# Compressing the past in eight units of two sequences, with pages issued without a loop and the bias from unsplit weights

## The chip, the cores and the metric

The kernel runs on one core of one Trainium2 chip. Five engines work at once on their own queues and meet at semaphores: TensorE (PE, matmuls), VectorE (DVE), ScalarE (ACT), GpSimd (POOL) and SyncE (SP, here an issuer of transfers). The metric is the device time of one execution in microseconds (us), less is better.

## What is computed

One inference step of a four-layer decoder for a prompt of 256 tokens and eight sequences with eight new tokens each, in float32. Four token mixers stand between eight feed-forward networks; their weights stream through the core once. This case is about one part of the last mixer (sparse attention): the eight sequences' past, 1024 rows each in pages of 128, is compressed to 63 keys and 63 values a sequence and group.

```python
def _nsa_compress(kf, w1, pe, w2):
    ...
    n_cmp = (tk - NSA_CMP_LEN) // NSA_CMP_STRIDE + 1
    sub = kf[:, :n_sub * NSA_CMP_STRIDE].reshape(b, n_sub, NSA_CMP_STRIDE, g, d)
    hid = 0.0
    for m in range(n_parts):
        rows = slice(m * NSA_CMP_STRIDE, (m + 1) * NSA_CMP_STRIDE)
        part = jnp.einsum('bnpgd,pdh->bngh', sub + pe[rows][:, None, :], w1[rows])
        hid = hid + part[:, m:m + n_cmp]
    return jax.nn.gelu(hid) @ w2

    past = cache_nsa_kv[page_table].reshape(b_s, past_len, 4, NSA_KV_HEADS, HEAD_DIM)
    ...
    k_cmp = _nsa_compress(full[:, :, 0], cmp_w1[0], cmp_pe[0], cmp_w2[0])
    v_cmp = _nsa_compress(full[:, :, 1], cmp_w1[1], cmp_pe[1], cmp_w2[1])
```

A hidden layer of 256 over windows of 32 rows (16 pairs of rows of 128 numbers), a gelu, and a second layer. The position term `pe` is the same for all windows, so its product with `w1` is a bias of the hidden layer.

## The kernel before, in words

The program does the past first, then x and the twelve stages, each of which takes its weights from one stream of chunks (`L264` issues one, `L290` and `L299` split it on ACT and DVE, `L317` multiplies). Matmuls run on float32r operands, so each float32 operand is split into a high part (a copy on ACT, rounded as it is written) and a low part (the remainder, on DVE), and a product is three matmuls: high with high, low weights with high, high weights with low.

The past is done in four *units*: unit 0 the keys and unit 1 the values of the first four sequences, units 2 and 3 those of the other four. A unit needs its pages (eight per sequence, 128 KB each) in `staged_pages`. SP issues those of sequences 0, 1 (and 4, 5), POOL those of 2, 3 (and 6, 7), both in a loop that reads a page number into a register and issues one transfer (`stage_pages`, `L1375` to `L1377`). `act_pairs` and `dve_pairs` turn the pages of a unit into `pair_hi` and `pair_lo`, four instructions of 512 columns a sequence pair on each engine; there are two slots, and unit u takes slot u modulo 2. `hidden_of` multiplies: two halves `ht` of the hidden layer, 16 row pairs, three products, 504 columns (63 windows, two groups, four sequences), 96 matmuls a unit. `act_gelu_past` adds the bias and takes the gelu out of PSUM, `keys` and `values` are the second layer on PE in plain float32 (two instructions a matmul), and `act_keep_past` copies their results.

The first-layer weights `w1` come in four pieces, by kind and by half of the hidden layer (16 row pairs of 128 columns); `act_w1_hi` and `dve_w1_lo` split each in two instructions. The bias is made on DVE in `dve_past`: 128 steps of 128 columns on the split weights, four accumulators in turn, between the pairs of unit 1 and those of units 2 and 3. Four matmuls with one column (`L1459`) sum it over the partitions, ACT copies it, and unit 2 waits for that copy.

The order of the work is written out by hand on each engine: `sp_past_first` and `sp_past_rest`, `pool_past`, `pe_past`, `act_past` (in three parts, with the scaling of x and the first weight splits between them) and `dve_past`. Stream chunks land where the pages of sequences 0 and 1 stood, the split weights where slot 0 stood, and `x_hi` where the pages of sequences 2 and 3 stood, so those steps wait for the units that read there.

## Time and profile before

| | us |
|---|---|
| median of 3 runs (lowest, highest) | 2662.05 (2661.71, 2663.11) |
| the profiled execution | 2664.5 |
| its span in the profile | 2662.8 |
| first matmul of the past | 39.66 |
| first matmul of the weight stream | 151.77 |
| PE busy over the span | 2534.2 (95%) |

The profile is of one execution. A timeline row gives an instruction's start in us from the start of the span, its length, engine, line, operation, what it writes and reads, and, in brackets, how long its engine stood idle ahead of it and what ended that. Buffer numbers are left out, so the four pieces of `w1` all read `w_raw`, `w_hi` and `w_lo`, as the stream's chunks do; the line tells them apart. Lengths of matmuls overlap: what one costs in a row of many is the distance between starts. PEld is the loading of weights.

### The profile page before, as it was taken

To read this page: it belongs to the slowest core of one execution; us is meant where nothing else is said; L and a number is where in the kernel's file an instruction comes from. 1 tells how busy PE (TensorE), PEld (TensorE's weight loads), DVE (VectorE), ACT (ScalarE), POOL (GpSimd) and SP (SyncE) were. 2 spreads that over 40 slices of the span, in tenths; PEclk is the share of its full clock that TensorE was granted. 3 is DMA by queue.
4 is the path that set the end of the run, shared out by engine and by line. 5 is a ranking of instruction groups with operands and counts; after the bars stand their busy time and mean duration, and the time that the engine had idled before them with its cause. 6 is when DMAs were issued, how large, how long until landed. Compare 5 with 4: busy or idle time off the path is not lost. (4 is left out here: it accounts for less than half of the span.)

```text
span 2662.8 us, 49610 instructions
## 1 busy us (share of the span) xinstructions
PE 2534.2 (95%) x17087; PEld 2450.5 (92%) x17087; DVE 1425.2 (54%) x2311; ACT 1327.5 (50%) x1979; POOL 790.3 (30%) x803
## 2 busy tenths in 40 slices
PE   4899998999999997999999999999999998889998
PEld 3799997999999995999999998999999997669998
DVE  5734545645455457555455456554454445756453
ACT  4445544455365436565366433564365333755552
POOL 2623312333133212333133214333133211113331
PEclk9999999999999997999999999999999998989999
DMA  7224344344444341344443443334444453214432
GB/s 221 70 95 157 135 150 145 111 158 139 152 151 146 142 185 37 111 150 146 146 158 142 146 154 143 140 144 150 150 144 156 146 216 111 64 47 143 156 137 106
DMA packets 73977, 366.13 MB, mean 137 GB/s; under 512 B 9154, under 2 KB 29954, under 8 KB 36482
## 3 DMA queue, kind: packets, MB, share of 16 engines
q1 hardware_dynamic: 72210, 356.58, 37.6%
q0 software_dynamic: 1536, 4.20, 0.5%
q10 hardware_dynamic: 144, 4.19, 0.4%
q8 instruction: 55, 0.90, 0.1%
q14 instruction: 32, 0.26, 0.0%
HBM read 361.98 MB, written 4.92 MB: 138 GB/s over the span
## 5 line engine op out<-in xcount | busy, mean ns | idle before, releaser
L317 PE MATMUL bank<-x_hi,w_hi 128*128 128x320 f32 x3336 | 1036.3, 311 | 0.0
L317 PE MATMUL bank<-x_lo,w_hi 128*128 128x320 f32 x3336 | 1032.0, 309 | 0.0
L317 PE MATMUL bank<-x_hi,w_lo 128*128 128x320 f32 x3336 | 1031.9, 309 | 0.0
L290 ACT ACTIVATE w_hi<-w_raw 128x1024 fp32r<-128x1024 f32 (+1 forms) x641 | 657.7, 1036 | 743.0 <-PE bank L317 724.2
L299 DVE TENSOR_TENSOR w_lo<-w_raw,w_hi 128x1024 fp32r<-128x1024 f32 (+1 forms) x641 | 828.7, 1328 | 263.9 <-ACT w_hi L290 263.9
L317 PEld LDWEIGHTS bank<-x_hi,w_hi 128*128 128x128 f32 x3336 | 626.5, 188 | 2.1 <-issue 0.7
L317 PEld LDWEIGHTS bank<-x_hi,w_lo 128*128 128x128 f32 x3336 | 626.5, 188 | 1.3
L317 PEld LDWEIGHTS bank<-x_lo,w_hi 128*128 128x128 f32 x3336 | 626.5, 188 | 0.0
L317 PE MATMUL bank<-h_hi,w_hi 128*128 128x320 f32 x1664 | 518.3, 311 | 8.9 <-POOL h_lo L843 6.5
L317 PE MATMUL bank<-h_hi,w_lo 128*128 128x320 f32 x1664 | 517.3, 311 | 0.0
L317 PE MATMUL bank<-h_lo,w_hi 128*128 128x320 f32 x1664 | 517.2, 311 | 0.0
L501 POOL TENSOR_TENSOR h<-silu,up 128x320 f32<-128x320 f32 x176 | 222.2, 1263 | 842.2 <-DVE up L430 837.2
L317 PEld LDWEIGHTS bank<-h_hi,w_hi 128*128 128x128 f32 x1664 | 315.0, 189 | 10.1 <-POOL h_lo L843 7.3
L317 PEld LDWEIGHTS bank<-h_hi,w_lo 128*128 128x128 f32 x1664 | 315.1, 189 | 0.0
L317 PEld LDWEIGHTS bank<-h_lo,w_hi 128*128 128x128 f32 x1664 | 314.8, 189 | 0.0
L488 POOL TENSOR_TENSOR sq<-x 128x320 f32 (+1 forms) x104 | 105.9, 1018 | 592.6 <-DVE x L450 591.9
L430 DVE TENSOR_TENSOR up<-bank,rstd 128x320 f32<-128x320 f32 x176 | 86.3, 492 | 303.2 <-PE bank L317 303.2
L430 DVE TENSOR_TENSOR gate_in<-bank,rstd 128x320 f32<-128x320 f32 x192 | 93.6, 491 | 271.1 <-PE bank L317 262.7
L506 POOL TENSOR_TENSOR h_lo<-h,h_hi 128x320 f32 x176 | 237.3, 1366 | 0.0
L375 ACT ACTIVATE x_hi<-x,gains (+1 forms) x96 | 53.4, 563 | 211.2 <-DVE x L450 206.9
L391 ACT ACTIVATE h_hi<-h 128x320 f32 x176 | 81.6, 464 | 96.5 <-POOL h L501 96.5
L450 DVE SCALAR_TENSOR_TENSOR x<-bank,x 128x320 f32 (+1 forms) x96 | 47.0, 490 | 142.0 <-PE bank L317 142.0
(283 smaller groups left out, 1936.0 us busy)
## 6 DMA issues: line engine op xcount, KB each, us to landing
w_raw<-stream SPq DMA_DIRECT2D x289, 1024.0 KB, 4.8
w_raw<-stream SPq DMA_DIRECT2D x32, 768.0 KB, 4.1
n_sel<-pool_sel SPq DMA_DIRECT2D x64, 128.0 KB, 2.2
w_raw<-cmp_w SPq DMA_DIRECT2D x4, 1024.0 KB, 7.5
pages<-pool_cmp POOLq DMA_DIRECT2D x32, 128.0 KB, 2.4
pages<-pool_cmp SPq DMA_DIRECT2D x32, 128.0 KB, 2.1
w_new<-cmp_w ACTq DMA_DIRECT2D x1, 4096.0 KB, 13.7
const<-const SPq DMA_DIRECT2D x1, 1533.0 KB, 8.0
```

Source lines behind the costliest of these rows:

```text
L290: act.activation(w_hi[:, (2 * n + half) % HALVES, 0:k, :], raw[:, n % RAW, 0:k, P * half:P * half + P], ACT.Copy).then_inc(hi_ready, 2 if ...
L299: dve.tensor_tensor(w_lo[:, s, 0:k, :], raw[:, n % RAW, 0:k, P * half:P * half + P], w_hi[:, s, 0:k, :].bitcast(F32), ALU.subtract).then_i ...
L317: mm = pe.matmul(acc, w[:, s, kk, :], a[:, k0 + kk, :], start=(first and kk == 0 and w is w_hi and a is act_hi), stop=(last and kk == k - ...
L375: act.activation(x_hi[:, bass.ds(m, 1), :], x[:, bass.ds(m, 1), :], ACT.Copy, scale=gains[:, norm, bass.ds(m, 1)]).then_inc(xhi_ready, 1)
L391: act.activation(h_hi[:, bass.ds(2 * i + f, 1), :], h[:, f:f + 1, :], ACT.Copy).then_inc(hhi_ready, 1)
L430: dve.tensor_tensor(dst, bank[g % BANKS][:, 0:T], rstd[:, :], ALU.mult).then_inc(evacuated, 1)
L450: dve.scalar_tensor_tensor(out=xm, in0=bank[g % BANKS][:, 0:T].rearrange("p (a t) -> p a t", a=1), scalar=scale, in1=xm, op0=ALU.mult, op1 ...
L488: pool.tensor_tensor(sq[:, :].rearrange("p (a t) -> p a t", a=1), x[:, bass.ds(m, 1), :], x[:, bass.ds(m, 1), :], ALU.mult).then_inc(ssum_ ...
L501: pool.tensor_tensor(h[:, f, :], silu[:, f, :], up[:, f, :], ALU.mult).then_inc(prod_ready, 1)
L506: pool.tensor_tensor(h_lo[:, t, :], h[:, f:f + 1, :], h_hi[:, t, :].bitcast(F32), ALU.subtract).then_inc(hlo_ready, 1)
```

## The change

The past is done in eight units of two sequences: units 2q and 2q + 1 are the keys and values of sequences 2q and 2q + 1, with SP issuing the even sequence's pages and POOL the odd one's. There are four pair slots, and unit u takes slot u modulo 4; slots 2 and 3 stand where the raw `w1` lay, so ACT waits for the bias steps before it fills them. A hidden matmul has 252 columns, and a unit still 96 of them, in two parts `c` of eight row pairs. `w1` is cut by kind and by row pairs, so that a piece is 8 KB a partition in one stretch. `stage_pages` reads its eight page numbers first and then issues eight transfers, without a loop. The bias is made from the raw weights, 256 columns wide, 16 steps for the keys and 16 for the values, each on the sum of the step before. PE starts with 24 matmuls on `w1_hi0` into a bank that is not read. Each `keys` or `values` is four matmuls of 128 columns and stands between the two parts of a later unit; hidden values have their own room for keys and values.

```diff
         def stage_pages(engine, q, i):
+            of_batch = [engine.value_load(pages[0:1, NPAGES * (2 * q + i) + r:NPAGES * (2 * q + i) + r + 1], min_val=0, max_val=n_pages - 1)
+                        for r in range(NPAGES)]
+            if q >= 2:
+                engine.wait_ge(pair_lo_ready, 2 * (2 * q - 3) + i + 1)
+            for r, pg in enumerate(of_batch):
+                engine.dma_start(staged_pages[q % 2][:, i, r:r + 1, :],
+                                 A["pool_cmp"][bass.ds(pg, 1)].rearrange("a p n -> p a n")).then_inc(staged[2 * (q % 2) + i], 16)
...
+        def sp_w1(sp, k):
+            sp.dma_start(w1_raw[k][:, :, :], A["cmp_w1"][:, k // 2, 8 * (k % 2):8 * (k % 2) + 8, :]).then_inc(past_w1_landed[k], 16)
...
             sp.wait_ge(pages_landed, 16)
-            for b in range(2):
-                stage_pages(sp, 0, b)
-            sp_w1(sp, 1)
+            stage_pages(sp, 0, 0)
+            for k in range(1, 4):
+                sp_w1(sp, k)
             sp.dma_start(cmp_pe[:, :, :], A["cmp_pe"]).then_inc(cmp_landed, 16)
+            stage_pages(sp, 1, 0)
             sp.dma_start(w2z[:, :, :, :, :], A["cmp_w2"]).then_inc(w2_landed, 16)
...
+        def hidden_of(pe, unit, c):
+            kv, slot, k = unit % 2, unit % 4, 2 * (unit % 2) + c
+            pe.wait_ge(w1_lo_ready, 2 * k + 2)
+            for ht in range(2):
+                out, col = bank[(2 * unit + ht) % 6][:, 0:4 * N_CMP_S], slice(P * ht, P * ht + P)
+                if c == 0 and unit >= 3:
+                    pe.wait_ge(hid_gelu, PRIME + 2 * (unit - 3) + ht + 1)
+                for pp in range(8):
+                    at = slice(4 * c, 4 * c + 4 * N_CMP_S)
+                    for w, a in ((w1_hi, pair_hi), (w1_lo, pair_hi), (w1_hi, pair_lo)):
+                        mm = pe.matmul(out, w[k][:, pp, col], a[slot][:, pp, at],
+                                       start=(c == 0 and pp == 0 and w is w1_hi and a is pair_hi),
+                                       stop=(c == 1 and pp == 7 and a is pair_lo))
...
+            pe.wait_ge(w1_hi_ready, 2)
+            for pp in range(24):
+                pe.matmul(bank[7][:, 0:256], w1_hi[0][:, pp % 8, 0:P], w1_hi[0][:, pp % 8, :], start=True, stop=True)
...
+            for unit in range(8):
+                pe.wait_ge(pair_lo_ready, 2 * unit + 2)
+                hidden_of(pe, unit, 0)
+                if unit == 2:
+                    pe.wait_ge(bias_step, 32)
...
+                if unit >= 3:
+                    if unit % 2:
+                        keys((unit - 3) // 2)
+                    else:
+                        values((unit - 4) // 2)
+                hidden_of(pe, unit, 1)
+            values(2)
+            keys(3)
+            values(3)
...
         def act_pairs(act, unit):
-            if unit >= 2:
-                act.wait_ge(hid_ready, 2 * (unit - 2) + 2)
+            if unit in (2, 3):
+                act.wait_ge(bias_step, 16 * (unit - 1))
+            if unit >= 4:
+                act.wait_ge(hid_ready, 2 * (unit - 4) + 2)
...
+        def dve_bias(dve, kv):
+            dve.wait_ge(cmp_landed, 16)
+            acc = bias_part[:, kv, :]
+            for pp in range(16):
+                src, pe_of = w1_raw[2 * kv + pp // 8][:, pp % 8, :], cmp_pe[:, kv, pp:pp + 1]
+                if pp == 0:
+                    dve.tensor_scalar(acc, src, pe_of, None, ALU.mult).then_inc(bias_step, 1)
+                else:
+                    dve.wait_ge(bias_step, 16 * kv + pp)
+                    dve.scalar_tensor_tensor(out=acc, in0=src, scalar=pe_of, in1=acc, op0=ALU.mult, op1=ALU.add)\
+                        .then_inc(bias_step, 1)
...
+            dve_w1_lo(dve, 0)
+            dve_pairs(dve, 0)
+            for k in range(1, 4):
+                dve_w1_lo(dve, k)
+            dve_pairs(dve, 1)
+            for kv in range(2):
+                dve_bias(dve, kv)
+                dve_pairs(dve, 2 + kv)
+            for unit in range(4, 8):
                 dve_pairs(dve, unit)
...
+                act_w1_hi(act, 0)
+                act_pairs(act, 0)
+                for k in range(1, 4):
+                    act_w1_hi(act, k)
+                for unit in range(1, 4):
                     act_pairs(act, unit)
                 act.wait_ge(bias_summed, 1)
...
-                    sp.wait_ge(pair_lo_ready, 12 + n + 1)
+                    sp.wait_ge(pair_lo_ready, 10 + n + 1)
```

Two places of the order. First SP, at the start of the program; `TENSOR_LOAD` reads a page number, `DMA` issues a transfer. Before, with a loop body that runs eight times:

```order
L1385 DMA page_table_66<-pages 1x64
L1382 DMA w1_raw0_121<-cmp_w1 128x16x128
L1382 DMA w1_raw1_122<-cmp_w1 128x16x128
L1376 TENSOR_LOAD page_table_66
L1376 ISA x2
L1377 ISA
L1377 DMA pages01_129<-pool_cmp 128x256
L1375 REGISTER_ALU
L1375 COMPARE_AND_BRANCH
```

With the change, where the two rows of the number and the two of the page stand eight times each:

```order
L1387 DMA page_table_66<-pages 1x64
L1384 DMA w1_raw0_129<-cmp_w1 128x2048
L1375 TENSOR_LOAD page_table_66
L1375 ISA x2
L1380 ISA
L1380 DMA pages01_133<-pool_cmp 128x256
L1384 DMA w1_raw1_130<-cmp_w1 128x2048
L1384 DMA w1_raw2_131<-cmp_w1 128x2048
L1384 DMA w1_raw3_132<-cmp_w1 128x2048
L1393 DMA cmp_pe_70<-cmp_pe 128x32
```

One piece of `w1` instead of two is issued ahead of the first batch, the page numbers are read in one go, and the other three pieces go out behind one batch, not two.

Then DVE, from the first weights to the pairs of the unit that follows the bias; `w1_lo` are remainders of weights, `pair_lo` those of pages. Before, where the step on four accumulators goes on for 128 instructions:

```order
L1489 TENSOR_TENSOR w1_lo0_117<-w1_raw0_121,w1_hi0_113 128x1024 x2
L1489 TENSOR_TENSOR w1_lo1_118<-w1_raw1_122,w1_hi1_114 128x1024 x2
L1498 TENSOR_TENSOR pair_lo0_128<-pages01_129,pair_hi0_127 128x512 x4
L1498 TENSOR_TENSOR pair_lo0_128<-pages23_130,pair_hi0_127 128x512 x4
L1489 TENSOR_TENSOR w1_lo2_119<-w1_raw2_123,w1_hi2_115 128x1024 x2
L1489 TENSOR_TENSOR w1_lo3_120<-w1_raw3_124,w1_hi3_116 128x1024 x2
L1498 TENSOR_TENSOR pair_lo1_126<-pages01_129,pair_hi1_125 128x512 x4
L1498 TENSOR_TENSOR pair_lo1_126<-pages23_130,pair_hi1_125 128x512 x4
L1517 TENSOR_SCALAR bias_part_131<-w1_hi0_113,cmp_pe_70 128x128
L1520 SCALAR_TENSOR_TENSOR bias_part_131<-w1_lo0_117,cmp_pe_70,bias_part_131 128x128
L1520 SCALAR_TENSOR_TENSOR bias_part_131<-w1_hi0_113,cmp_pe_70,bias_part_131 128x128
L1498 TENSOR_TENSOR pair_lo0_128<-pages01_129,pair_hi0_127 128x512 x4
```

With the change:

```order
L1496 TENSOR_TENSOR w1_lo0_117<-w1_raw0_129,w1_hi0_113 128x1024 x2
L1505 TENSOR_TENSOR pair_lo0_122<-pages01_133,pair_hi0_121 128x512 x4
L1496 TENSOR_TENSOR w1_lo1_118<-w1_raw1_130,w1_hi1_114 128x1024 x2
L1496 TENSOR_TENSOR w1_lo2_119<-w1_raw2_131,w1_hi2_115 128x1024 x2
L1496 TENSOR_TENSOR w1_lo3_120<-w1_raw3_132,w1_hi3_116 128x1024 x2
L1505 TENSOR_TENSOR pair_lo1_124<-pages01_133,pair_hi1_123 128x512 x4
L1515 TENSOR_SCALAR bias_part_135<-w1_raw0_129,cmp_pe_70 128x256
L1518 SCALAR_TENSOR_TENSOR bias_part_135<-w1_raw0_129,cmp_pe_70,bias_part_135 128x256 x7
L1518 SCALAR_TENSOR_TENSOR bias_part_135<-w1_raw1_130,cmp_pe_70,bias_part_135 128x256 x8
L1505 TENSOR_TENSOR pair_lo2_126<-pages23_134,pair_hi2_125 128x512 x4
L1515 TENSOR_SCALAR bias_part_135<-w1_raw2_131,cmp_pe_70 128x256
L1505 TENSOR_TENSOR pair_lo3_128<-pages23_134,pair_hi3_127 128x512 x4
```

The pairs of unit 0 need one row of four instructions and stand ahead of three of the four weight pieces, and the bias is cut in two with the pairs of unit 2 between the halves.

## Rows read from the trace of the kernel before

**Rows 1.** Timeline, PE, 0 to 152 us: start us, length us, engine, line, operation, tiles, shape, count.

```profile
39.66 0.79 PE L1423 MATMUL bank<-pair_hi,w_hi 128*128 128x504 f32 x1 [39.66 <-DVE pair_lo L1498]
...
43.45 0.39 PE L1423 MATMUL bank<-pair_hi,w_hi 128*128 128x504 f32 x1
...
52.30 0.39 PE L1423 MATMUL bank<-pair_hi,w_hi 128*128 128x504 f32 x1
...
86.76 1.10 PE L1459 MATMUL bank<-one_col,bias_part 128*128 128x1 f32 x8 [1.44 <-DVE bias_part L1520]
...
119.84 3.71 PE L1450 MATMUL bank<-w2z,past_hid 128*63 128x128 f32 x32
...
151.77 0.42 PE L317 MATMUL bank<-x_hi,w_hi 128*128 128x320 f32 x1
```

**Rows 2.** Two stretches: length, busy us of each engine, PEclk, DMA share, GB/s.

```profile
0.00:39.60 39.60, 0.00 (x0) 0.00 (x0) 12.95 (x14) 15.61 (x16) 8.98 (x21) 1.00 0.79 224
...
85.30:94.70 9.40, 1.11 (x9) 1.02 (x9) 9.40 (x15) 6.78 (x8) 9.40 (x1) 0.62 0.00 1
```

**Rows 3.** Timeline, PE, 399.7 to 402.1 us, inside the weight stream.

```profile
399.80 0.31 PE L317 MATMUL bank<-x_hi,w_hi 128*128 128x320 f32 x1
...
402.00 0.31 PE L317 MATMUL bank<-x_hi,w_hi 128*128 128x320 f32 x1
```

**Rows 4.** Timeline, weight loads of PE (PEld), 85 to 88 us.

```profile
86.76 1.01 PEld L1459 LDWEIGHTS bank<-one_col,bias_part 128*128 128x128 f32 x8 [1.88 <-DVE bias_part L1520]
```

**Rows 5.** Timeline, SP, three windows of one batch of pages each.

```profile
4.78 12.75 SPq L1377 DMA_DIRECT2D pages<-pool_cmp  x8
...
2238.71 3.99 SPq L1584 DMA_DIRECT2D n_sel<-pool_sel  x8
...
2248.11 4.49 SPq L1584 DMA_DIRECT2D n_sel<-pool_sel  x8
```

**Rows 6.** Timeline, POOL, 0 to 130 us: its first page and its eighth.

```profile
4.01 0.71 POOL L1377 DMA_DIRECT2D pages<-pool_cmp  x1 [3.40 <-issue]
...
14.74 0.54 POOL L1377 DMA_DIRECT2D pages<-pool_cmp  x1 [0.98 <-issue]
```

**Rows 7.** The page's DMA issues: count, KB each, median us to landing.

```profile
w_raw<-stream SPq DMA_DIRECT2D x289, 1024.0 KB, 4.8
...
w_raw<-cmp_w SPq DMA_DIRECT2D x4, 1024.0 KB, 7.5
...
pages<-pool_cmp POOLq DMA_DIRECT2D x32, 128.0 KB, 2.4
...
pages<-pool_cmp SPq DMA_DIRECT2D x32, 128.0 KB, 2.1
```

**Rows 8.** Groups of 0 to 152 us: count | busy us, mean ns | idle before.

```profile
L1480 ACT ACTIVATE pair_hi<-pages 128x512 fp32r<-128x512 f32 x32 | 35.2, 1195 | 36.2 <-DMA pages<-pool_cmp 23.3 <-PE bank L1423 12.9
...
L1498 DVE TENSOR_TENSOR pair_lo<-pages,pair_hi 128x512 fp32r<-128x512 f32 x32 | 34.1, 1149 | 16.9 <-ACT pair_hi L1480 16.9
...
L1520 DVE SCALAR_TENSOR_TENSOR bias_part<-w_lo,cmp_pe,bias_part 128x128 f32<-128x128 f32 x64 | 17.9, 333 | 0.0
...
L1489 DVE TENSOR_TENSOR w_lo<-w_raw,w_hi 128x1024 fp32r<-128x1024 f32 x8 | 9.3, 1222 | 8.1 <-ACT w_hi L1470 8.1
...
L423 DVE SCALAR_TENSOR_TENSOR x_lo<-x,gains,x_hi 128x320 fp32r<-128x320 f32 x8 | 8.1, 1079 | 0.7 <-ACT x_hi L375 0.7
...
L1531 ACT ACTIVATE past_hid<-bank,cmp_bias 128x504 f32<-128x504 f32 x8 | 5.1, 679 | 25.2 <-PE bank L1450 13.0 <-PE bank L1423 10.1 <-PE bank L1441 2.1
...
L1531 ACT ACT_TABLE_LOAD x1 | 1.3, 1283 | 0.0
```

**Rows 9.** Groups of the whole span, DVE: a wide and a chained instruction.

```profile
L547 DVE SCALAR_TENSOR_TENSOR x<-x,gains,rstd 128x320 f32<-128x320 f32 x8 | 3.8, 548 | 0.0
...
L1953 DVE SCALAR_TENSOR_TENSOR n_hit<-n_imp,n_low,const 128x14 f32<-128x14 f32 x8 | 1.9, 234 | 0.3
```

More of the change, by code:

```diff
@@ L1279, in program @@
             staged = [sem(f"staged{b}") for b in range(4)]
+            past_clear = sem("past_clear")
             w1_hi_ready = sem("w1_hi_ready")
@@ L1413, in hidden_of @@
-        def hidden_of(pe, unit, ht, out):
-            kv = unit % 2
-            hi, lo = pair_hi[unit % 2], pair_lo[unit % 2]
-            for pp in range(16):
-                if unit < 2:
-                    if pp % 8 == 0:
-                        pe.wait_ge(w1_lo_ready, 4 * kv + 2 * ht + pp // 8 + 1)
-                at = slice(8 * (pp // 8), 8 * (pp // 8) + 8 * N_CMP_S)
-                for w, a in ((w1_hi, hi), (w1_lo, hi), (w1_hi, lo)):
-                    mm = pe.matmul(out, w[2 * kv + ht][:, pp, :], a[:, pp % 8, at], start=(pp == 0 and w is w1_hi and a is hi),
-                                   stop=(pp == 15 and a is lo))
-            return mm
@@ L1427, in pe_past @@
-        def pe_past(pe):
-            def unit(u, then=(None, None)):
-                pe.wait_ge(pair_lo_ready, 4 * u + 4)
-                if u == 3:
-                    pe.wait_ge(hid_gelu, PRIME + 2)
-                for ht in range(2):
-                    hidden_of(pe, u, ht, bank[(2 * u + ht) % 6][:, 0:8 * N_CMP_S]).then_inc(hid_ready, 1)
-                    if then[ht]:
-                        then[ht](u - 2)
-            def keys(half):
-                pe.wait_ge(hid_gelu, PRIME + 4 * half + 2)
-                pe.wait_ge(cmp_kept, PRIME + 2 * half - 1)
+            for q in range(4):
+                stage_pages(pool, q, 1)
@@ L1442, in keys @@
                                    start=(k == 0), stop=(k == 3))
                 mm.then_inc(cmp_made, 1)
-            def values(half):
-                pe.wait_ge(hid_gelu, PRIME + 4 * half + 4)
-                pe.wait_ge(cmp_kept, PRIME + 2 * half)
-                for b in range(4):
-                    for k in range(4):
-                        mm = pe.matmul(bank[7][0:N_CMP_S, P * b:P * b + P],
-                                       past_hid[:, k // 2, k % 2, N_CMP_S * b:N_CMP_S * b + N_CMP_S],
-                                       w2z[:, 1, k // 2, k % 2, :], start=(k == 0), stop=(k == 3))
-                mm.then_inc(cmp_made, 1)
@@ L1455, in pe_past @@
-            unit(0)
-            unit(1)
-            pe.wait_ge(bias_step, 128)
-            for k in range(4):
-                mm = pe.matmul(bank[6][:, k:k + 1], bias_part[:, k, :], one_col[:, :], start=True, stop=True)
-            mm.then_inc(bias_summed, 1)
-            pe.wait_ge(w2_landed, 16)
-            pe.wait_ge(bias_ready, 1)
-            unit(2, (keys, values))
-            unit(3, (keys, values))
-        def act_w1_hi(act, kv):
-            for ht in range(2):
-                act.wait_ge(past_w1_landed[2 * kv + ht], 16)
-                for c in range(2):
-                    act.activation(w1_hi[2 * kv + ht][:, 8 * c:8 * c + 8, :], w1_raw[2 * kv + ht][:, 8 * c:8 * c + 8, :], ACT.Copy)\
-                        .then_inc(w1_hi_ready, 1)
@@ L1473, in act_pairs, with values @@
-        def act_pairs(act, unit):
-            if unit >= 2:
-                act.wait_ge(hid_ready, 2 * (unit - 2) + 2)
-            for b in range(4):
-                act.wait_ge(staged[b], 16 * NPAGES * (unit // 2 + 1))
-                out, src = pairs_of(pair_hi[unit % 2], b), staged_of(unit, b)
+            def values(q):
+                pe.wait_ge(hid_gelu, PRIME + 4 * q + 4)
+                pe.wait_ge(cmp_kept, PRIME + 2 * q)
+                for k in range(4):
+                    mm = pe.matmul(bank[7][:, 0:P], past_hid[:, 1, k // 2, k % 2, :], w2z[:, 1, k // 2, k % 2, :],
+                                   start=(k == 0), stop=(k == 3))
+                mm.then_inc(cmp_made, 1)
```

160 lines of the change are left out of this document (79 added, 81 removed).

## The prediction

> **What bounds the kernel now.** I read the stretches first, then TensorE's (PE) timeline, then what each wait on it ends on. Everything the change touches lies before 151.77 us, where the first matmul of the weight stream starts [rows 1]; after it the program is unchanged, so only that start can move. PE does nothing until 39.66 and stands nearly empty from 85.30 to 94.70 [rows 1, 2]; the rest of the stretch is matmuls without a break. The first gap ends on `pair_lo` from VectorE (DVE), which needs all four sequences' pages; the second ends on `pair_lo` of unit 2, which DVE makes only after the whole bias chain. So the stretch has three prices: a late head, a gap in the middle, and the matmuls themselves.
>
> **The matmuls.** 384 of 504 columns become 768 of 252. Thirty-nine starts of 504 columns cover 8.85 us [rows 1], 0.227 each; fifteen starts of 320 columns cover 2.20 us [rows 3], 0.147 each. The line through both, 0.436 ns a column, gives 0.117 us at 252. That is one bound. The other is the weight load, for the number of loads doubles: eight loads with one-column matmuls took 1.01 us [rows 4], so at most 0.126 each. I take 0.117, since at 0.147 and 0.227 the load is wholly hidden and the stream still (barely) exceeds it. 768 x 0.117 = 89.9 us against 384 x 0.227 = 87.2: 2.7 us dearer, or 9.6 by the other bound. A unit of 96 matmuls is 11.2 us. Keys and values were four groups, now eight of 4 matmuls with 128 columns; 16 such matmuls (32 instructions) took 3.71 us [rows 1], so 0.93 a group.
>
> **The head.** A batch of eight pages took SP 12.75 us in the loop. The same work without a loop stands at the end of the trace: eight issues in 3.99 us, and 2248.11 - 2242.70 = 5.41 us of reading eight page numbers ahead of the next eight [rows 5]: 9.4 us. POOL's first page went out at 4.01 [rows 6]; one page number (5.41 / 8 = 0.68) earlier, at 3.3, the table was there. SP's batch is then issued by 12.7 and lands 2.1 later [rows 7], at 14.8. POOL's: its loop spaced pages by (14.74 - 4.01) / 7 = 1.53 us [rows 6]; without the loop eight issues cost between SP's 4.0 and 8 x 1.53 - 5.4 = 6.8, since its number reads may take no less. Landing takes 2.4, so 15.1 to 18.0; I take 16.5. Unit 0 needs these two batches alone, not four. ScalarE (ACT) then needs two instructions of 35.2 / 32 = 1.10 us, DVE two of 34.1 / 32 = 1.07 [rows 8]: PE starts at 20.8 instead of 39.66. The weights of w1 now come in 8 KB rows, the shape of a stream chunk, which lands in 4.8 us where the old 512-byte rows took 7.5 [rows 7]; the three later ones are issued from 12.7 on, and DVE wants the last at about 24. I cost them at nothing while that holds. The 24 added warm-up matmuls run before 20.8 on an idle PE; I give them no gain, because PE idles again between them and the first pages. The first nine matmuls took 3.79 us where nine later ones take 2.04 [rows 1]; I keep these 1.75 us.
>
> **The bias chain and the gap.** 128 instructions on the split weights (64 of them 17.9 us [rows 8]) become 32 of twice the width on the raw ones. But there were four accumulators in turn, and now each instruction waits for the one before it. Width 256 lies two thirds of the way from 333 ns (128 wide, [rows 8]) to 548 (320 wide, [rows 9]): 0.476, plus 0.3 / 8 = 0.04 for a wait on DVE's own last result [rows 9]: 0.516. Pipelined it would be 17.9 / 64 = 0.28 and 3.8 / 8 = 0.475, so 0.41. I take 0.516 because the wait is in the code: 16 steps are 8.3 us for each of keys and values. The raw weights lie under slots 2 and 3, so ACT may fill those slots only after each half of the chain; queued behind that wait on ACT are pairs(3), the bias copy and gelu(0).
>
> Walked through, on DVE: 20.8; six weight remainders of 9.3 / 8 = 1.16 [rows 8] to 27.8; pairs(1), 4 x 1.07, to 32.1; bias of the keys to 40.4; pairs(2), where ACT does 4 x 1.10 and DVE 2 x 1.07 behind it, to 46.9; bias of the values to 55.2; pairs(3) to 61.7. On PE: unit 0 from 20.8 to 33.8 (cold start included), unit 1 to 45.0, a wait of 1.9 for pairs(2), first half of unit 2 to 52.5, a wait of 2.7 for the bias, the four bias matmuls 1.0 [rows 4], second half to 61.8. Unit 3 finds its pairs; gelu(0), after ACT's pairs(3) at 59.6, a table load of 1.28 and half of 0.68 [rows 8], frees its bank at 61.6. Units 3 to 7 at 11.2 + 0.93 follow without a wait, because ACT and DVE need 6.5 us for the pairs of a unit that lasts 12.2: 122.7. Two values groups, one keys group, and a gelu of 0.68 between: 126.2. The x work (DVE 8.1 us, [rows 8]) and the first weight splits hide behind units 6 and 7; if that cover were gone they would cost up to these 8.1. The page issues of the later batches wait for pairs(1) and pairs(3), 20 us before use: nothing.
>
> **Sum.** The stream starts at 126.2 instead of 151.77: 25.6 us less. The profiled execution took 2664.5 us (span 2662.8); 2664.5 - 25.6 = 2638.9. The median of the runs, 2662.05, lies 2.4 below that execution, so I predict 2636. No change can be told from 0.2%, 5.3 us.
>
> **Rivals.**
> A, *the head is bound by transfer, not by issue*. The first 39.6 us moved 224 GB/s with the DMA engines 0.79 busy [rows 2]. If 224 stays, four weight pieces and the first two batches, 6 MB, are in at 28. Taken in the order of issue only the last weights are late: pairs(1) and the chain behind it slip by some 4 us, 2640. If all share alike, unit 0 starts at 32: 2647. For it: the busy share; against it: nearly half of that traffic was w1 in 512-byte rows. 0.15.
>
> B, *POOL's pages come no faster unrolled*: 1.53 us a page stays and the number reads come on top, 3.3 + 5.4 + 12.3 + 2.4 = 23.4 instead of 16.5. Then the change does not do what it says on one of two queues, 2643. 0.07.
>
> C, *slower: the weight load stands beside the short matmul, not under it*. Place: the hidden layer's line, 768 times. Price: 252 columns of 0.436 ns and a load of 0.126 make 0.236, 768 x 0.119 = 91 us more: 2727. It decides from 0.117 + 26 / 768 = 0.151 us on; above that the change is slower. Against it: a pair of load and 320 columns would be 0.140 + 0.126 = 0.266, and 0.147 is measured [rows 3]. For it: no matmul of this kind under 320 columns is in the trace, and plain float32 at 128 columns costs 3.71 / 16 = 0.232 [rows 1]; at that rate 252 columns would be 0.457, some 260 us more, which I keep out of the range. 0.08.
> The Trainium skill (TensorE: Matmul & The Clock Gate, section "The mechanism") says that weight loads overlap matmuls in flight only where the row group differs, and its section on LDWEIGHTS gives columns / 1.2 ns, 107 ns here; an estimate by these pages would be 0.217 us a matmul, some 2713. All loads of the stream use all rows, and the trace's 0.147 does not agree with the first statement.
>
> **How the numbers follow.** Forecast 0.70, A 0.15, B 0.07, C 0.08. The forecast's own ends: pipelined bias steps (twice 1.9) and POOL at its early end (1.4) give 2631, faster pairs perhaps 2627; matmuls at 0.126 (+6.9) and POOL late (+1.5) give 2645. With A to 2647 and B the range is 2627 to 2650. All but C are faster; of C and of several small slips together I give 0.04 to no change.
>
> **What would show it.** Right: the first hidden matmul near 21, starts 0.117 apart, bias steps near 0.52, two waits of 2 to 3 us around unit 2, the stream near 126. A: ACT waiting on w1 or pages after 18. B: POOL's pages 1.5 apart. C: starts 0.15 apart or more. Wrong altogether: a stream start that moves by 25 us while the end does not, which would mean that later stages wait for something that the past covered.

## The result: 2643.24 us, and the profile after

The changed kernel takes 2643.24 us (median of 5 runs, 2641.17 to 2649.82), the kernel before on the same chip 2663.11 (5 runs, 2661.71 to 2670.32): a ratio of 0.9918, 95% interval 0.9899 to 0.9938, so faster by 0.6 to 1.0%. Single times of one kernel lie up to 9 us apart. The sign and the range of the prediction held; its number, 2636, was 7.2 us too low.

The profiled execution took 2643.24 us with a span of 2641.1, against 2664.5 and 2662.8. Its stretches, with the columns of [rows 2]:

```profile
5.60:8.00 2.40, 0.00 (x1) 0.00 (x1) 0.97 (x1) 2.00 (x2) 0.30 (x1) 1.00 0.00 0
8.00:21.00 13.00, 5.42 (x24) 5.19 (x24) 3.53 (x4) 3.69 (x4) 7.73 (x15) 0.83 0.96 332
...
23.90:26.80 2.90, 2.90 (x13) 2.90 (x14) 2.90 (x3) 2.10 (x3) 0.00 (x0) 0.50 1.01 340
...
50.80:54.10 3.30, 3.30 (x18) 3.30 (x17) 3.08 (x7) 0.00 (x0) 0.00 (x0) 0.50 0.00 0
...
54.20:129.30 75.10, 73.63 (x631) 73.07 (x631) 37.89 (x41) 40.81 (x60) 22.80 (x25) 1.00 0.23 76
```

The third number from the end is the clock that PE was granted (0.50 is 1.2 GHz, 1.00 is 2.4), the one behind it the share of the DMA engines. These stand still from 5.6 to 8.0 us, while SP and POOL read page numbers, and are nearly full from 8.0 to about 40. PE is busy for 98% of the time from 54.2 to the stream.

TensorE's timeline, which answers to [rows 1]:

```profile
8.00 5.42 PE L1435 MATMUL bank<-w_hi 128*128 128x256 f32 x24 [8.00 <-ACT w_hi L1478]
23.88 0.58 PE L1426 MATMUL bank<-pair_hi,w_hi 128*128 128x252 f32 x1 [10.46 <-DVE pair_lo L1505]
...
27.09 0.28 PE L1426 MATMUL bank<-pair_hi,w_hi 128*128 128x252 f32 x1
...
28.25 0.28 PE L1426 MATMUL bank<-pair_hi,w_lo 128*128 128x252 f32 x1
...
50.42 0.39 PE L1426 MATMUL bank<-pair_hi,w_hi 128*128 128x252 f32 x1 [2.59 <-DVE pair_lo L1505]
...
58.49 1.05 PE L1460 MATMUL bank<-one_col,bias_part 128*128 128x1 f32 x8 [0.66 <-DVE bias_part L1518]
...
65.49 0.38 PE L1426 MATMUL bank<-pair_hi,w_hi 128*128 128x252 f32 x1 [0.26 <-DVE pair_lo L1505]
...
128.41 1.13 PE L1450 MATMUL bank<-w2z,past_hid 128*128 128x128 f32 x8 [0.56 <-ACT vcmp_s L1553]
129.30 0.39 PE L317 MATMUL bank<-x_hi,w_hi 128*128 128x320 f32 x1
```

The first hidden matmul comes at 23.88 instead of 39.66, the nine-microsecond hole of [rows 2] is now two short waits at 50.42 and 58.49, and the stream starts at 129.30 instead of 151.77. From 27.09 to 28.25 there are ten steps of 0.116 us; unit 3 to unit 7 keep 0.117.

The DMA issues, as in [rows 7], then the first issues on SP and on POOL, then ScalarE and VectorE, whose rows show the chain that unit 3 waits for:

```profile
w_raw<-cmp_w SPq DMA_DIRECT2D x4, 1024.0 KB, 9.8
...
pages<-pool_cmp SPq DMA_DIRECT2D x32, 128.0 KB, 4.8
...
pages<-pool_cmp POOLq DMA_DIRECT2D x32, 128.0 KB, 5.1
```

```profile
7.14 3.97 SPq L1380 DMA_DIRECT2D pages<-pool_cmp  x8
11.16 1.59 SPq L1384 DMA_DIRECT2D w_raw<-cmp_w  x3
...
18.72 4.55 SPq L1380 DMA_DIRECT2D pages<-pool_cmp  x8
```

```profile
7.70 4.64 POOL L1380 DMA_DIRECT2D pages<-pool_cmp  x8 [7.14 <-issue]
17.13 4.63 POOL L1380 DMA_DIRECT2D pages<-pool_cmp  x8 [4.79 <-issue]
```

```profile
16.33 2.15 ACT L1489 ACTIVATE pair_hi<-pages 128x512 fp32r<-128x512 f32 x2 [8.38 <-DMA pages<-pool_cmp]
19.46 2.20 ACT L1489 ACTIVATE pair_hi<-pages 128x512 fp32r<-128x512 f32 x2 [0.98 <-DMA pages<-pool_cmp]
...
26.25 2.01 ACT L1478 ACTIVATE w_hi<-w_raw 128x1024 fp32r<-128x1024 f32 x2 [0.80 <-DMA w_raw<-cmp_w]
...
43.46 4.77 ACT L1489 ACTIVATE pair_hi<-pages 128x512 fp32r<-128x512 f32 x4 [10.45 <-DVE bias_part L1518]
58.47 4.65 ACT L1489 ACTIVATE pair_hi<-pages 128x512 fp32r<-128x512 f32 x4 [10.24 <-DVE bias_part L1518]
```

```profile
23.72 6.91 DVE L1496 TENSOR_TENSOR w_lo<-w_raw,w_hi 128x1024 fp32r<-128x1024 f32 x6
30.66 4.71 DVE L1505 TENSOR_TENSOR pair_lo<-pages,pair_hi 128x512 fp32r<-128x512 f32 x4
...
35.65 7.78 DVE L1518 SCALAR_TENSOR_TENSOR bias_part<-w_raw,cmp_pe,bias_part 128x256 f32<-128x256 f32 x15
45.86 4.50 DVE L1505 TENSOR_TENSOR pair_lo<-pages,pair_hi 128x512 fp32r<-128x512 f32 x4 [2.43 <-ACT pair_hi L1489]
...
50.66 7.78 DVE L1518 SCALAR_TENSOR_TENSOR bias_part<-w_raw,cmp_pe,bias_part 128x256 f32<-128x256 f32 x15
60.75 4.68 DVE L1505 TENSOR_TENSOR pair_lo<-pages,pair_hi 128x512 fp32r<-128x512 f32 x4 [2.32 <-ACT pair_hi L1489]
```

From 23.72 to 65.43 VectorE stops only twice, for the 2.4 us in which ScalarE makes the first half of a slot. The pages of the first unit are there at 16.33 and 19.46, and ScalarE waits for pages and weights in turn. The medians 4.8 and 5.1 are over all the pages; of the first two batches, SP's was issued by 11.11 and POOL's by 12.34, so their last pages came 5.2 and 7.1 us after their issue. The pages of the next two sequences, which ScalarE does not read before 43.46, are issued at 17.13 and 18.72, while the last weights are still on their way.

Where the time came from: span -21.7 us, stream start -22.5, everything behind it +0.8 (2511.8 against 2511.0). That the last two agree so well is in part chance, for this stretch scatters by some 10 us between traces, as the last experiment shows. By the medians the change is worth 19.9 us, and 17.9 in the repeat at the end.

### The profile page after: what moved, and what is told of

It reads as the page before. It is cut to its first block and busy times, and to the rows that moved or that the text cites. A ratio compares the mean times of both kernels' runs of the same rounds, so it can differ in the third digit from the quotient of the medians.

```text
span 2641.1 us, 50131 instructions
## 1 busy us (share of the span) xinstructions
PE 2538.1 (96%) x17479; PEld 2471.5 (94%) x17479; DVE 1408.2 (53%) x2216; ACT 1331.9 (50%) x1995; POOL 767.8 (29%) x802
## 5 line engine op out<-in xcount | busy, mean ns | idle before, releaser
L488 POOL TENSOR_TENSOR sq<-x 128x320 f32 (+1 forms) x104 | 82.4, 792 | 594.0 <-DVE x L450 593.3
```

The lines of the kernel that those rows point to most:

```text
L488: pool.tensor_tensor(sq[:, :].rearrange("p (a t) -> p a t", a=1), x[:, bass.ds(m, 1), :], x[:, bass.ds(m, 1), :], ALU.mult).then_inc(ssum_ ...
```

## The experiments

Theory T: the head is bound by the 6 MB of pages and weights that VectorE needs up to the pairs of unit 1, and from there VectorE's chain (remainders, pairs, bias, pairs, bias, pairs) sets when unit 3 starts; behind that TensorE is the bound. Rival I: the issuing of the pages sets the head. Rival P: TensorE's own matmuls set the stretch from the start. The single runs are compared by the start of the stream, since their times carry some 10 us of scatter. The start of the stream itself came 1.8 us later when the changed kernel was profiled again, so the start of the four bias matmuls (`L1460`, behind VectorE's second bias) is given beside it where the difference is small; a table at the end has both for all the kernels.

**The page loop put back.**

```diff
-            for r, pg in enumerate(of_batch):
-                engine.dma_start(staged_pages[q % 2][:, i, r:r + 1, :],
+            with engine.Fori(0, NPAGES) as r:
+                pg = engine.value_load(pages[0:1, bass.ds(r + NPAGES * (2 * q + i), 1)], min_val=0, max_val=n_pages - 1)
+                engine.dma_start(staged_pages[q % 2][:, i, bass.ds(r, 1), :],
```

> The changed kernel with the page loop put back (read one page number, issue one page, branch), all else as changed. There the first hidden matmul starts at 23.9 us and the weight stream at 129.3. Theory T (the pages are bound by transfer from 8 us on, and the DMA engines idle while eight numbers are read first): pages start near 4 us, 1.5 apart on each queue, land by 17.5, first hidden matmul near 22, stream near 127.3. Theory I (the prediction's: the head is set by how long a batch takes to issue, 12.75 against 9.4 us): first hidden matmul near 27, stream near 132.5.

Measured: first hidden matmul at 25.42 (+1.5), stream at 131.80 (+2.5), 2649.93 us. ScalarE, waiting for the two batches:

```profile
15.99 2.15 ACT L1488 ACTIVATE pair_hi<-pages 128x512 fp32r<-128x512 f32 x2 [7.70 <-DMA pages<-pool_cmp]
21.03 2.15 ACT L1488 ACTIVATE pair_hi<-pages 128x512 fp32r<-128x512 f32 x2 [2.89 <-DMA pages<-pool_cmp]
```

SP's batch lands no later than with the change, POOL's 1.6 us later, and the bias matmuls start 1.5 us later (59.96 against 58.49). The other 1.0 us of the 2.5 lies behind them, where the clock is at 0.50 from 62.3 to 65.8. So issuing without a loop is worth some 1.5 us of the 22.5, on POOL's queue alone. Both forecasts missed: T had the loop 2 us faster than the change, rival I 3.2 us slower.

**Each page issued as soon as its number is read.** Still no loop, but number and transfer in turn, so the DMA engines don't stand still at 5.6.

```diff
-            of_batch = [engine.value_load(pages[0:1, NPAGES * (2 * q + i) + r:NPAGES * (2 * q + i) + r + 1], min_val=0, max_val=n_pages - 1)
-                        for r in range(NPAGES)]
...
-            for r, pg in enumerate(of_batch):
+            for r in range(NPAGES):
+                at = NPAGES * (2 * q + i) + r
+                pg = engine.value_load(pages[0:1, at:at + 1], min_val=0, max_val=n_pages - 1)
```

> The changed kernel without a loop, but each page issued right after its number is read. Theory T: pages start near 3 us instead of 7.1, the idle of the DMA engines is filled, first hidden matmul near 20.5 (now 23.9), and since DVE's chain hangs on it, the stream 3 us earlier, near 126. Theory I: reads and issues take the same sum, the last page goes out at the same time, first matmul 23.9 and stream 129.3 within 0.7.

Measured: first hidden matmul at 23.21 (-0.7), stream at 130.40 (+1.1), 2644.82 us. ScalarE:

```profile
14.19 2.15 ACT L1489 ACTIVATE pair_hi<-pages 128x512 fp32r<-128x512 f32 x2 [5.92 <-DMA pages<-pool_cmp]
18.82 2.15 ACT L1489 ACTIVATE pair_hi<-pages 128x512 fp32r<-128x512 f32 x2 [2.48 <-DMA pages<-pool_cmp]
...
23.80 2.00 ACT L1478 ACTIVATE w_hi<-w_raw 128x1024 fp32r<-128x1024 f32 x2 [0.94 <-DMA w_raw<-cmp_w]
27.54 2.01 ACT L1478 ACTIVATE w_hi<-w_raw 128x1024 fp32r<-128x1024 f32 x2 [1.73 <-DMA w_raw<-cmp_w]
```

The pages are there 2.1 and 0.6 us earlier, the last weights 1.3 later. In the six traces of kernels that issue the head as the changed kernel does, the two batches were there at 15.2 to 16.9 and at 18.9 to 19.7, the last weights at 25.1 to 26.8; so SP's gain and the weights' loss are outside the scatter, POOL's 0.6 is not. VectorE, which needs both, reaches the bias 1.2 us later (36.48 against 35.28). My expectation from T was wrong in its numbers, because it let the pages gain and forgot the weights behind them; the trade itself speaks for T. Rival I missed the stream too, and the end of the issue does not set the landing: SP had issued its eight pages by 11.1, 14.3 and 11.2 us in the changed kernel, with the loop and here, and they were there at 16.3, 16.0 and 14.2.
The Trainium skill (Trainium Kernel Development and Optimization, section "Key Constraints") says that transfers issued from different engines share the same DMA engines, so that more issuers save issue time only; the trade between pages and weights agrees.

**No warm-up matmuls.** Nothing reads their result.

```diff
-            for pp in range(24):
-                pe.matmul(bank[7][:, 0:256], w1_hi[0][:, pp % 8, 0:P], w1_hi[0][:, pp % 8, :], start=True, stop=True)
```

> The changed kernel without the 24 matmuls that warm the array up (their result is not read). Theory T: the granted clock is back at 0.5 before the first page is split and DVE's chain, not PE, sets when unit 3 starts, so first hidden matmul 23.9 and stream 129.3 within 0.5. Theory W (the warm-up pays): the stream 1.5 us later or more.

Measured: first hidden matmul at 23.40 (-0.5), stream at 129.79 (+0.5), 2645.55 us. No gain or loss that can be told. In the changed kernel the clock is at 0.50 when unit 0 starts, after 10.46 us without a matmul, and rises at 26.9. Without the warm-up the matmuls stand 0.21 us apart until 28.9, as they do at 0.50:

```profile
23.40:28.90 5.50, 5.50 (x26) 5.50 (x27) 5.50 (x5) 4.88 (x6) 0.00 (x0) 1.00 1.07 351
```

The clock column reads 1.00 in this row; the 26 matmuls in 5.50 us do not agree with it. VectorE's chain sets the start of the bias matmuls in either case (57.96 here, 58.49 with the warm-up). Behind them the clock is at 0.50 from 59.6 to 63.1 here, which is why the stream is the later one.

**Two bias accumulators.** Even and odd row pairs are summed apart, and the four bias matmuls become eight that add up.

```diff
+                acc = bias_part[:, kv, pp % 2, :]
...
-                    dve.wait_ge(bias_step, 16 * kv + pp)
+                    dve.wait_ge(bias_step, 16 * kv + pp - 1)
```

> The changed kernel with two bias accumulators a kind in turn, so that a step waits for the one before the last; four more one-column matmuls. Theory T (DVE's chain sets the start of unit 3, and a bias step costs 0.52 us only because it waits for the last): steps 0.41 apart, each half 1.7 us shorter, pairs(3) and unit 3 3.4 earlier, stream near 126. Theory P (the matmuls set the stream's start, the bias is hidden): stream 129.3 within 0.5. Theory S (a step of this width takes 0.52 anyhow): steps 0.52 apart, stream unchanged.

Measured: stream at 125.93 (-3.4), 2642.22 us. VectorE and TensorE:

```profile
35.84 5.62 DVE L1519 SCALAR_TENSOR_TENSOR bias_part<-w_raw,cmp_pe,bias_part 128x256 f32<-128x256 f32 x14
```

```profile
54.73 1.95 PE L1461 MATMUL bank<-one_col,bias_part 128*128 128x1 f32 x16 [0.20 <-DVE bias_part L1519]
...
125.93 0.39 PE L317 MATMUL bank<-x_hi,w_hi 128*128 128x320 f32 x1
```

A step falls from 0.52 us (7.78 / 15) to 0.40 (5.62 / 14), a half of the bias from 8.1 to 6.1. The bias matmuls start 3.8 us earlier (54.73), which is nearly both halves' 4.0, and 3.4 of it reach the stream. PE now goes from 23.80 to the bias matmuls almost without a wait. So the dependent accumulation, which the change brought in, was on the path, as T says.

**The bias from the split weights again**, 64 dependent steps of 256 columns.

```diff
-                src, pe_of = w1_raw[2 * kv + pp // 8][:, pp % 8, :], cmp_pe[:, kv, pp:pp + 1]
+                for e, w in enumerate((w1_hi, w1_lo)):
+                    step = 2 * pp + e
+                    src, pe_of = w[2 * kv + pp // 8][:, pp % 8, :].bitcast(F32), cmp_pe[:, kv, pp:pp + 1]
```

> The changed kernel with the bias taken from the split weights again: 64 dependent steps of 256 columns on VectorE instead of 32, everything else as changed. Theory T (the vector engine's chain pairs(1), bias, pairs(2), bias, pairs(3) sets when unit 3 starts): each half of the bias lasts 16.3 us instead of 8.1, so pairs(2) and pairs(3) come 8 and 16 us later, the stream starts near 145.8 instead of 129.3 and the time is near 2660. Rival P (TensorE's own matmuls set the stretch, the bias hides beside them): the stream start moves by under 3 us, the time stays under 2647.

Measured: stream at 147.24, 2660.36 us. PE's waits are now:

```profile
58.26 0.58 PE L1426 MATMUL bank<-pair_hi,w_hi 128*128 128x252 f32 x1 [9.57 <-DVE pair_lo L1505]
...
74.66 1.87 PE L1460 MATMUL bank<-one_col,bias_part 128*128 128x1 f32 x8 [8.60 <-DVE bias_part L1520]
```

16.6 us of added steps (32 x 0.52) move the bias matmuls by 16.2 and the stream by 17.9; the clock is at 0.50 from 69.3 to 79.6. A microsecond on VectorE's chain is one on the end, and with a dependent chain of twice the length nearly the whole change would be gone. This also says that the early head alone is worth little: with it, but with a bias of 33 us, the stream starts only 4.5 us before that of the kernel before. What the short bias alone would give there, no run shows.

**The page issue without a loop, alone, in the kernel before.**

```diff
+            of_batch = [engine.value_load(pages[0:1, NPAGES * (4 * half + b) + r:NPAGES * (4 * half + b) + r + 1], min_val=0, max_val=n_pages - 1)
+                        for r in range(NPAGES)]
...
-            with engine.Fori(0, NPAGES) as r:
-                pg = engine.value_load(pages[0:1, bass.ds(r + NPAGES * (4 * half + b), 1)], min_val=0, max_val=n_pages - 1)
-                engine.dma_start(staged_pages[b // 2][:, b % 2, bass.ds(r, 1), :],
+            for r, pg in enumerate(of_batch):
+                engine.dma_start(staged_pages[b // 2][:, b % 2, r:r + 1, :],
```

> The kernel before with one part of the change alone: pages issued without a loop, eight numbers read first. Before, the first hidden matmul is at 39.66 and the stream at 151.77. Theory issue (the loop's 1.5 us a page sets the head): each queue's two batches are issued by 22 to 25 us instead of 30, first hidden matmul near 33, stream near 146, time near 2657. Theory transfer (the first stretch moved 224 GB/s with its engines 0.79 busy, so an earlier issue only queues): the first hidden matmul gains 3 us or less, stream at 148 or later, time 2659 or more.

Measured: first hidden matmul at 34.98 (-4.7), stream at 148.05 (-3.7), 2657.86 us. Between the two theories: 32 pages are many enough for the loop to matter, and the landing takes 3.6 (SP) and 3.4 us (POOL) instead of 2.1 and 2.4 [rows 7], which eats part of it. The other 18.8 us, if the parts add up, lie in the rest of the change (half as many pages ahead of the first matmul, a bias of 32 steps cut in two), which was not taken apart further.

**A long warm-up**, with two bias accumulators.

```diff
-            for pp in range(24):
+            for pp in range(110):
```

> The run with two bias accumulators, and 110 warm-up matmuls instead of 24, so that TensorE is busy from 8 to about 23 us, up to the first hidden matmul near 23.8. Theory T (with the bias off the path, the cold clock of unit 0 is what is left: its matmuls lose some 2.3 us against full clock): the granted clock is 1.0 through unit 0, the stream starts near 123.6 instead of 125.9, time near 2640. Rival: the clock falls all the same, or the start is late by the warm-up's tail: the stream stays at 125.9 or later.

Measured: stream at 127.70, 2640.39 us. Two stretches, the wait that came up, and VectorE's pairs of unit 3:

```profile
13.50:46.90 33.40, 32.96 (x279) 32.62 (x278) 24.71 (x33) 19.99 (x18) 8.58 (x16) 1.00 0.94 348
...
57.90:61.20 3.30, 3.30 (x18) 3.30 (x17) 3.27 (x4) 3.27 (x6) 0.00 (x0) 0.50 0.13 38
```

```profile
48.91 0.38 PE L1426 MATMUL bank<-pair_hi,w_hi 128*128 128x252 f32 x1 [1.74 <-DVE pair_lo L1506]
```

```profile
57.16 4.53 DVE L1506 TENSOR_TENSOR pair_lo<-pages,pair_hi 128x512 fp32r<-128x512 f32 x4 [2.24 <-ACT pair_hi L1490]
```

The clock stays at 1.00 through units 0 and 1, as wanted, and they take 23.1 us (23.84 to 46.9) instead of 23.7. PE then only waits for `pair_lo` of unit 2, so the bias matmuls start no earlier (54.97 against 54.73 with 24 warm-up matmuls). T's 123.6 was wrong: VectorE's chain was still just behind. Some 9 us after that wait the clock falls to 0.50, from 57.8 to 61.3, at a place where PE is the bound, and that is the 1.8 us by which the stream is later.

**The weights held back** until POOL's first pages are in, with pages issued one by one, two accumulators, 80 warm-up matmuls.

```diff
             stage_pages(sp, 0, 0)
+            sp.wait_ge(staged[1], 16 * NPAGES)
             for k in range(1, 4):
                 sp_w1(sp, k)
```

> Two bias accumulators, each page issued as soon as its number is read, the last three weight pieces held back on SP until POOL's first eight pages have landed, 80 warm-up matmuls. Theory T (the head is bound by transfers shared by pages and weights): without the weights beside them the pages land near 14 to 16 us, not 18.8, the first hidden matmul is near 20, the weights land some 3 us later, and the stream starts near 120 to 123. Rival I (issue sets the landing): pages land at 18 to 19 as before, first hidden matmul at 23 or later; and if the held weights are late for units 1 and the bias, the stream starts at 126 or later.

Measured: SP's pages in at 14.38, POOL's by 14.69, where SP's wait for them ends and the weights go out, first hidden matmul at 21.35, last weights at 28.33, stream at 127.51, 2648.67 us. With the weights beside them POOL's pages were there at 18.82 (pages issued in the same way, above): so the weights cost them 4 us, as T says. But the weights are late now, and unit 1 waits 4.16 us:

```profile
14.69 1.29 SPq L1384 DMA_DIRECT2D w_raw<-cmp_w  x3
```

```profile
36.97 0.58 PE L1427 MATMUL bank<-pair_hi,w_hi 128*128 128x252 f32 x1 [4.16 <-DVE pair_lo L1507]
```

In this order what the pages gain the weights lose again. POOL's second batch goes out from 13.24 on, ahead of the weights, though ScalarE does not read it before 43.01; holding that back instead was not tried.

**One weight piece earlier, then finer reports.** The second weight piece (1 MB) is issued straight behind the first, into the 2.4 us in which the DMA engines stood still, with two accumulators and 94 warm-up matmuls. The second of these kernels also lets ScalarE report each pair instruction, not every second.

```diff
             sp_w1(sp, 0)
+            sp_w1(sp, 1)
             sp.wait_ge(pages_landed, 16)
...
-                    o = act.activation(out[:, :, grp], src[:, :, grp], ACT.Copy)
-                o.then_inc(pair_hi_ready, 1)
+                    act.activation(out[:, :, grp], src[:, :, grp], ACT.Copy).then_inc(pair_hi_ready, 1)
...
+                    dve.wait_ge(pair_hi_ready, 4 * unit + 2 * i + grp + 1)
```

> The run with two bias accumulators and a long warm-up, and SP issues the second weight piece (1 MB) straight behind the first, ahead of the page numbers, into the 2 us in which the transfer engines stand idle; 94 warm-up matmuls. Theory T (the head is bound by the 6 MB of pages and weights that VectorE needs by pairs(1)): filling the idle time brings pages no later and the last weight piece some 2 us earlier; the chain from the weight remainders to pairs(2) moves 1 to 2 us earlier, first hidden matmul at 22 to 23.8, stream at 125.7 to 126.7 against 127.7. Rival (the order of the page issues alone sets the head): weights and chain stay, stream 127.7 or, if the pages come later behind the weights, up to 129.

> As the run with the early weight piece, and ScalarE reports each of its four pair instructions instead of every second, so that VectorE starts on a slot after 1.15 us instead of 2.3. Theory T (VectorE's chain still sets when units 2 and 3 start): pairs(2) and pairs(3) come 1.1 and 2.3 us earlier, TensorE finds unit 2 nearly without a wait, the stream starts at 123.5 to 125, the time is 2637 to 2640. Rival P (TensorE's own matmuls set the stretch now): the stream stays where the run with the early weight piece alone has it.

Measured: with the piece alone, pages in at 16.28 and 19.54, no wait of ScalarE for weights any more, stream at 126.12 against 127.70, 2642.87 us. TensorE at unit 0 and VectorE at the pairs of unit 3:

```profile
24.20 0.58 PE L1427 MATMUL bank<-pair_hi,w_hi 128*128 128x252 f32 x1 [1.86 <-DVE pair_lo L1507]
```

```profile
57.16 4.75 DVE L1507 TENSOR_TENSOR pair_lo<-pages,pair_hi 128x512 fp32r<-128x512 f32 x4 [2.29 <-ACT pair_hi L1491]
```

The stream is where T wanted it, but not for T's reason. VectorE's pairs of unit 3 start at 57.16 with the early piece and without it. From the first of its six weight remainders to the bias matmuls the chain takes 30.85 us, against 31.25 with the long warm-up and 31.07 with two accumulators alone: 0.2 to 0.4 us, not 1 to 2. The 1.6 us against the long warm-up are the clock's: it is at 0.50 from 24.2 to 27.7 here, where PE waits for VectorE afterwards anyway (0.51 us at unit 2), and not behind the bias matmuls.

With the finer reports too, stream at 124.75, 2640.45 us (5 runs), ratio 0.9910 to before (0.9893 to 0.9927). Stretches of the second:

```profile
5.60:8.00 2.40, 0.00 (x0) 0.00 (x0) 0.76 (x1) 1.85 (x2) 0.48 (x1) 1.00 0.96 397
8.00:21.00 13.00, 12.79 (x85) 12.79 (x86) 4.92 (x5) 4.78 (x5) 7.73 (x15) 1.00 0.99 341
```

Filling the hole costs the pages nothing that can be told, and ends ScalarE's waits for weights. With the finer reports VectorE's waits for units 2 and 3 fall from 2.47 and 2.29 us to 1.31 and 1.21, and its pairs of unit 3 start at 53.18 instead of 57.16: some 3.2 us by three such waits, 0.8 because POOL's pages happened to come sooner (18.78). The bias matmuls start 2.9 us earlier than with the piece alone (52.02 against 54.92), and the stream gains 1.4 of it: there PE is the bound, and its clock is at 0.50 from 54.9 to 58.4.

**The changed kernel and the best one once more, on one chip.**

> The changed kernel itself once more, unedited, on the same chip as the run beside it, to see how far its time and its stream start repeat. Theory T (what is left after the stream start scatters by some 4 us with the granted clock of later stages, the stretch before it does not): stream start within 1 us of 129.3, median 2641 to 2645.

> The run with two bias accumulators, long warm-up, early weight piece and finer reports, unedited, beside the changed kernel on the same chip. Theory T: stream start within 1.5 us of 124.75, so 4.5 us earlier than the changed kernel's, and the median 3 to 6 us under it. Rival (a head start of this size is lost again in a later stage that waits for something else): the two medians within 1.5 us.

Measured, 6 runs each: the changed kernel 2645.04 us (2642.80 to 2651.93), 0.9932 of before (0.9915 to 0.9949), stream at 131.11; the best one 2640.12 (2637.32 to 2645.18), 0.9904 (0.9888 to 0.9920), stream at 124.48. The medians are 4.9 us apart, as T had it, though the two intervals still touch. The changed kernel's stream start does not repeat within 1 us as expected: it came 1.8 us later, though the bias matmuls started 0.8 us earlier (57.70), because the clock fell to 0.50 from 58.2 to 64.9, in the second half of unit 2 and in unit 3, and not at 50.8, where VectorE was behind anyway:

```profile
58.20:64.90 6.70, 6.70 (x32) 6.70 (x33) 4.41 (x4) 6.67 (x9) 0.00 (x0) 0.50 0.19 53
```

So a difference of less than 2 us between two stream starts says nothing by itself. The marks on the way, for all the variants of the changed kernel, in us:

| kernel | six weight remainders start | bias matmuls start | clock at 0.50 behind that | stream starts |
|---|---|---|---|---|
| changed | 23.72 | 58.49 | no | 129.30 |
| changed, again | 23.12 | 57.70 | to 64.9 | 131.11 |
| page loop put back | 25.26 | 59.96 | 62.3 to 65.8 | 131.80 |
| page by page | 23.06 | 59.80 | no | 130.40 |
| no warm-up | 23.26 | 57.96 | 59.6 to 63.1 | 129.79 |
| split weights | 23.98 | 74.66 | to 79.6 | 147.24 |
| two accumulators | 23.66 | 54.73 | no | 125.93 |
| and long warm-up | 23.72 | 54.97 | 57.8 to 61.3 | 127.70 |
| weights held back | 21.19 | 56.31 | no | 127.51 |
| early weight piece | 24.07 | 54.92 | no | 126.12 |
| and finer reports | 22.31 | 52.02 | 54.9 to 58.4 | 124.75 |
| the same, again | 22.02 | 51.76 | 53.8 to 57.3 | 124.48 |

The bias matmuls start within 0.1 us of the end of VectorE's second bias in every kernel but one (page by page, 0.3). From there to the stream it is 70.6 to 71.2 us where the clock stays at 1.00, and 71.8 to 73.4 where it falls. VectorE's chain is thus shown to be the bound up to the bias matmuls; behind them TensorE and its clock set the rest, and unit 3 itself waited for VectorE in one trace alone, the first of the changed kernel, by 0.26 us.

The program behind the stream start is the same in every kernel here, yet took 2508.1 us (pages unrolled alone) to 2518.9 (weights held back) in the profiled executions. The whole of it in the last two runs, first the changed kernel, then the best one:

```profile
131.10:2640.50 2509.40, 2431.72 (x16618) 2365.42 (x16616) 1335.62 (x2130) 1268.21 (x1914) 732.25 (x749) 0.98 0.39 138
```

```profile
124.50:2643.30 2518.80, 2440.82 (x16618) 2372.97 (x16616) 1336.31 (x2130) 1268.12 (x1914) 731.64 (x749) 0.97 0.39 138
```

The same 16618 matmuls keep PE busy 9.1 us longer, at a clock of 0.97 instead of 0.98, and the stretch is 9.4 us longer. That is as much as the single times above scatter; why the clock differs there was not tried. By chance the profiled execution of the changed kernel is the fastest of its six, that of the best one the slowest.

## Why the prediction was right, and where it was short

| | forecast | measured |
|---|---|---|
| first two batches of pages in | 14.8, 16.5 | 16.33, 19.46 |
| first hidden matmul | 20.8 | 23.88 |
| start to start of a hidden matmul | 0.117 | 0.117 |
| half of the bias | 8.3 | 8.1 |
| waits at unit 2 | 1.9, 2.7 | 2.59, 0.66 |
| unit 3 starts | 61.8 | 65.49 |
| unit 3 to the end of unit 7 | 60.9 | 60.4 |
| stream starts | 126.2 | 129.30 |
| profiled execution | 2638.9 | 2643.24 |

**The matmuls** were right to the last digit, though not for all the reason given: the load's bound of 0.126 lies above 0.117, so it did not follow that the columns exceed the load. Rival C is out: the weight load stays under a matmul of 252 columns. The Trainium skill's statement in "The mechanism" (TensorE: Matmul & The Clock Gate) that loads overlap only where the row group differs is not what these rows show, for all loads here use all rows; the estimate by that page was 2713.

**The bias chain** was right as the bound and in its size, and both sides of its price were measured: 0.52 us a step as the code stands, 0.40 with two sums, the lower bound that the prediction gave as 0.41. Two slips in the working change nothing: 16 such steps save 1.7 us a half, not 1.9, and gelu(0) frees its bank at 61.2 by the terms given, not 61.6.

**The head** is the step that failed. The prediction let the last page of a batch land 2.1 and 2.4 us after its issue, from a kernel in which pages went out 1.5 us apart, and costed the three weight pieces at nothing. The issue was over sooner than forecast (at 11.1 and 12.3 us instead of 12.7 and 14.1), but the last pages came 5.2 and 7.1 us after it, the weights took 9.8 instead of 4.8, and the DMA engines were nearly full from 8 us on. For POOL's batch the cause is shown: with the weights held back it was there 4 us sooner. For SP's batch no run takes it apart. This is rival A's mechanism and its sign in the trace, ScalarE waiting on pages and weights after 18. VectorE's chain began 2.9 us late and passed this on, to 3.1 at the stream. That rival A's 2640 to 2647 holds the result is partly luck: it went by 224 GB/s and had the last weights in at 28, and measured were 332 GB/s from 8 to 21 us, behind 2.4 us without any transfer, and the last weights at 26.25. So the likeliest case was right in what lies behind the head, and A in what bounds the head.

The prediction overlooked two things in the head. Reading eight numbers first leaves the DMA engines idle; the early weight piece showed that this can be filled, but also that it gains only 0.2 to 0.4 us on VectorE's chain. And the pages of the next two sequences, 2 MB that nobody reads for another 25 us, share the DMA engines with the last weights; no run held them back.

**Rival B** is out: eight pages from POOL took 4.64 us instead of eight times 1.53. **The warm-up** gave nothing, as forecast, and for the reason given. **The waits at unit 2** add up (3.3 us and 1.5 of slow clock against 4.6): the clock fell behind the first wait and stretched the first half of unit 2 to 7.1 us, beside VectorE's work. In the repeat, where it did not fall there, they were 1.86 and 2.21.

**The number**: 7.2 us short are 3.1 of the stream start, 0.8 behind it, 0.4 outside the span, and 2.9 from taking the median 2.4 us (and rounding) below the profiled execution, which of the changed kernel is the median itself. The small 0.8 is luck, given the scatter of that stretch. What the clock takes between the bias matmuls and the stream is no term of the prediction at all; in the repeat it made the stream start at 131.11.

## What to carry to other kernels

A landing time read where transfers are spaced out does not hold once they are issued faster: add up the bytes that the first work needs, and look for the stretches in which the DMA engines stand still. Bytes put there cost the others nothing here, but they gained little, because the pages still came last. When an accumulation is rewritten with fewer instructions, count its dependent steps against the independent ones it replaces, and keep two sums if it is on the path. Removing a wait on TensorE pays only as far as the engine that feeds it has slack; check the feeder's rows before buying a warmer clock. And compare two runs at the last point that the edited chain sets, not at a later one that the clock moves too: the early weight piece looked like 1.6 us at the stream and was 0.2 to 0.4 on the chain.

## What the runs showed of the hardware that was not expected

- What the clock was when unit 0 started: after 24 warm-up matmuls from 8.0 to 13.4 and 10.46 us without one it was at 0.50; after 94 matmuls and 1.86 us (early weight piece) it was too; after 80 and 1.27 us, after 94 and 0.18 or 0.39 us, and after 110 without a wait, it was at 1.00.
- TensorE's clock also fell to 0.50, for 3 to 7 us, behind waits at unit 2, but not at a fixed distance: at once in the first trace of the changed kernel (wait 2.59 us), some 9 us after the wait with the long warm-up (1.74) and with finer reports (0.77), and not at all with the early weight piece alone (0.51). What decides it stays open.
- The 1 MB put into the idle stretch moved at 397 GB/s and delayed the pages by nothing that can be told (16.28 and 19.54 with the early piece alone, against 16.33 and 19.46).
